# Block transposes on VectorE in the RWKV recurrence, and two gate projections moved into neighbouring jobs

## What is computed

```python
# first layer: 3592 columns of w_in; the last 8 are f_c, one per head
q_a, f_a, i_a, g_a, u_b, g_b, q_c, k_c, v_c, g_c, f_c = jnp.split(proj, IN_SPLIT_POINTS, axis=-1)
log_f_c = jax.nn.log_sigmoid((f_c + fox_f_bias[l]).astype(jnp.float32))
...
# second layer, RWKV: 16 heads of 64
def step(state, inp):
    r_t, w_t, k_t, v_t, a_t, b_t = inp
    sa = jnp.einsum('bhvk,bhk->bhv', state, a_t)
    state = (state * w_t[:, :, None, :] + sa[..., None] * b_t[:, :, None, :]
             + v_t[..., None] * k_t[:, :, None, :])
    return state, jnp.einsum('bhvk,bhk->bhv', state, r_t)
...
# second layer, NSA: the last 48 of its columns are gates (3 per head)
gates = jax.nn.sigmoid(gl.astype(f32)).reshape(B, S, G, HG, 3).transpose(0, 2, 3, 1, 4)
```

## Time and profile before

| | |
|---|---|
| time, median of 3 runs | 1584.03 us (1581.96 to 1585.93) |
| the profiled execution | 1581.26 us |
| its span | 1579.5 us |
| PE busy in the span | 1532.5 us (97%) |
| DVE / ACT / POOL busy | 894.6 / 695.7 / 120.6 us |
| mean granted TensorE clock | 0.992 |

### The profile page before, as it was taken

How to read it: one execution, slowest core, us unless ns; L and a number is a source line. 1 busy time by engine, 2 the same in 40 slices (tenths; PEclk the granted TensorE clock), 3 DMA queues, 4 the chain that set the end, 5 groups by cost and what they waited for, 6 DMA issues and landing times.

```text
span 1579.5 us, 33484 instructions
## 1 busy us (share of the span) xinstructions
PE 1532.5 (97%) x14426; PEld 1266.6 (80%) x14426; DVE 894.6 (57%) x1651; ACT 695.7 (44%) x1268; POOL 120.6 (8%) x86
## 2 busy tenths in 40 slices
PE   7999999899999999999999999999999999999998
PEld 6787867779789797897887677888887888888887
DVE  3658364656474574842245998433246677777323
ACT  5543264563352633524234998423235333333222
POOL 0004000002230322302000000000000000000000
PEclk9999989999999999999999999999999999999999
DMA  6322212431020110206312000223332323323231
GB/s 222 108 81 81 93 41 100 158 107 37 16 68 11 54 36 17 67 11 149 80 54 80 2 2 2 94 83 104 107 134 93 107 81 107 105 83 107 77 121 70
DMA packets 110978, 124.40 MB, mean 79 GB/s; under 512 B 21320, under 2 KB 94664, under 8 KB 110448
## 3 DMA queue, kind: packets, MB, share of 16 engines
q1 hardware_dynamic: 107904, 114.85, 23.1%
q10 hardware_dynamic: 2928, 7.41, 1.4%
HBM read 118.04 MB, written 4.21 MB: 77 GB/s over the span
## 4 chain that ended last, share of the span: by engine, by line
PE 84%; DVE 9%; ACT 5%; issue 2%; POOL 0%; DMA 0%; DVEq 0%; SPq 0%; ACTq 0%; POOLq 0%
PE bank L807 80%; PE bank L817 4%; ACT arena L1487 3%; DVE arena L2098 2%; DVE arena L2095 2%; DVE weights_lo L2095 1%; ACT L1487 1%; DVE arena L2102 1%; ACT weights_hi L1487 1%; DVE arena L2270 1%; DVE arena L2462 0%; DVE extra L2095 0%; DVE arena L2188 0%; DMA arena<-in_x 0%; ACT extra L1487 0%
## 5 line engine op out<-in xcount | busy, mean ns | idle before, releaser
L1487 ACT ACTIVATE arena<-bank 128x512 f32<-128x512 f32 (+3 forms) x415 | 225.3, 569 | 554.4 <-PE bank L807 528.0
L2095 DVE TENSOR_TENSOR weights_lo<-weights,weights_hi 128x1024 fp32r<-128x1024 f32 (+1 forms) x190 | 239.3, 1260 | 304.6 <-ACT weights_hi L1487 297.4
L807 PE MATMUL bank<-h_hi,weights_hi 128*128 128x512 f32 (+1 forms) x1008 | 400.8, 398 | 4.1 <-DVE h_lo L2098 1.9
L807 PE MATMUL bank<-h_lo,weights_hi 128*128 128x512 f32 (+1 forms) x1008 | 393.9, 391 | 0.0
L807 PE MATMUL bank<-h_hi,weights_lo 128*128 128x512 f32 (+1 forms) x1008 | 393.9, 391 | 0.0
L807 PE MATMUL bank<-arena 64*64 64x64 f32 (+6 forms) x7746 | 344.0, 247 | 14.7 <-DVE arena L2098 5.9
L807 PEld LDWEIGHTS bank<-arena 64*64 64x64 f32 (+3 forms) x7746 | 281.0, 140 | 68.2 <-issue 57.2
L1487 ACT ACTIVATE weights_hi<-weights 128x1024 fp32r<-128x1024 f32 (+1 forms) x190 | 200.1, 1053 | 172.3 <-PE bank L807 169.5
L807 PEld LDWEIGHTS bank<-h_hi,weights_hi 128*128 128x128 f32 (+1 forms) x1008 | 189.9, 188 | 50.8 <-issue 6.9
L807 PEld LDWEIGHTS bank<-h_hi,weights_lo 128*128 128x128 f32 (+1 forms) x1008 | 189.9, 188 | 40.6
L807 PEld LDWEIGHTS bank<-h_lo,weights_hi 128*128 128x128 f32 (+1 forms) x1008 | 190.0, 188 | 37.5
(11 more groups left out here) (172 smaller groups left out, 1628.2 us busy)
## 6 DMA issues: line engine op xcount, KB each, us to landing
weights<-in_w_in SPq DMA_DIRECT2D x39, 1024.0 KB, 5.3
weights<-in_ffn_up SPq DMA_DIRECT2D x22, 1024.0 KB, 5.1
weights<-in_ffn_down SPq DMA_DIRECT2D x10, 1024.0 KB, 5.0
weights<-in_w_out SPq DMA_DIRECT2D x8, 1024.0 KB, 5.0
weights<-in_w_in SPq DMA_DIRECT2D x16, 256.0 KB, 4.4
weights<-in_w_branch_rwkv SPq DMA_DIRECT2D x4, 1024.0 KB, 5.2
weights<-in_w_branch_nsa SPq DMA_DIRECT2D x4, 1024.0 KB, 5.2
weights<-in_w_in SPq DMA_DIRECT2D x5, 512.0 KB, 3.7
```

Of the source, the lines that this page charges most:

```text
L807: return pe.matmul(o, w, x, start=first, stop=last)
L1487: return act.activation(o, i, f, **kw)
L2095: return dve.tensor_tensor(o, a, b, op)
```

## The change

It has three parts.

1. In the RWKV solve the transposed powers are no longer made by matmuls. DVE transposes 32x32 blocks instead (`dve.transpose`, in the rows STREAM_TRANSPOSE, 128x512 each): `pw_even` into `ba` (twice per quarter), the results of `pa` 0 and `pa` 1 out of PSUM into `pwt` (four times), and `invt` into `inv` (four times). The jobs `pb`, `mx` and `mz` go, 8 groups of PE per quarter; `gram` loses the 64 columns from which `ba` was masked (384 instead of 512 per job). `bonus` moves behind `pa` 0. ACT's copy of `pa` 0 and 1 waits for DVE's transpose of the same bank.
2. The job `fc0` goes. Its 8 columns join the job `i` (264 columns); ACT copies them beside the values, and 4 small matmuls with the identity turn them (job `fc`, after `hk`). The gates' steps move from after `f0`, `q1` and `gb0` to after `i`, `gc0` and `gc1`, and SP's store and reload from ahead of `gc2`'s weights to ahead of `qc0`'s. The slots grow from 2048 to 2112 words, the pieces from 1024 to 1056.
3. The NSA gate job goes. Its 48 columns take 48 of the third lora job's 96 unused ones; ACT keeps them by one more copy (`keep`).

```diff
-        tokens(base["p1", "i"], w1, 512, 256)
+        tokens(base["p1", "i"], w1, None, 256 + FOX_HEADS, runs=((0, 512, 256), (256, 3584, FOX_HEADS)))
...
-        channels(base["lora"] + 2, (0, cols(w2, RWKV_COLS - P, RWKV_COLS)))
+        nb = RWKV_COLS
+        channels(base["lora"] + 2, (0, cols(w2, nb + 2560, nb + 2608)), (48, cols(w2, nb - 80, nb)))
...
-                if n == use_of[base["p1", "gc2"]]:
+                if n == use_of[base["p1", "qc0"]]:
...
-                    to_tokens(base["p1", name], h_both, 256)
+                    to_tokens(base["p1", name], h_both, 256 + FOX_HEADS)
                     pe.wait_ge(sem("hg_scaled"), 2)
                     for n in range(2):
                         transposes(base["hk"] + n, [hg_k[:, n, c * P:(c + 1) * P] for c in range(TT)])
+                    for i in range(TT):
+                        wait_read(pe, base["p1", "i"] + i)
+                    claim(pe, base["fc"])
+                    for i in range(TT):
+                        ins = mm(ps(base["fc"])[0:FOX_HEADS, i * P:(i + 1) * P], fc_tok[:, i, :], ident)
+                    fill(base["fc"], ins)
                 elif name == "v":
...
+                            at_ = 192 * n + DH * m
                             for x in range(2):
...
-                                    ins = mm(ps(j)[z, at_:at_ + P], src[both[x], n, tok], a_r[both[x], n, c, :, z])
+                                    if m:
+                                        ins = mm(ps(j)[z, at_:at_ + P], src[both[x], n, tok], a_r[both[x], n, c, :, z])
+                                    else:
+                                        ins = mm(ps(j)[z, at_:at_ + DH], src[both[x], n, tok], a_r[both[x], n, c, 1, z])
...
+
+                for g in range(2):
+                    pe.wait_ge(sem("powers_turned"), 6 * q + g + 1)
+                    pair_of_tiles(J[q, "pa", g, 0], g, ba, pw_even)
                 by_head(J[q, "bonus"], t1_q)
-
-
-                for g in range(2):
-                    pe.wait_ge(sem("powers_started"), 2 * q + g + 1)
-                    for c in (2 * g, 2 * g + 1):
-                        for x in range(2):
-                            wait_read(pe, J[q, "gram", c, x])
-                    pair_of_tiles(J[q, "pa", g, 0], g, ba, pw_even)
-                    pair_of_tiles(J[q, "pb", g, 0], g, pw_even, ba)
                 for g in range(2):
                     wait_read(pe, J[q, "pa", g, 0])
-                    wait_read(pe, J[q, "pb", g, 0])
+                    pe.wait_ge(sem("powers_turned"), 6 * q + g + 3)
                     pair_of_tiles(J[q, "pa", g, 1], g, pwt, pw_odd)
-                    pair_of_tiles(J[q, "pb", g, 1], g, pw_odd, pwt)
                     pe.wait_ge(sem("inv_started"), 2 * q + g + 1)
...
                 for g in range(2):
                     wait_read(pe, J[q, "pa", g, 1])
-                    wait_read(pe, J[q, "pb", g, 1])
+                    pe.wait_ge(sem("powers_turned"), 6 * q + g + 5)
                     pair_of_tiles(J[q, "pa", g, 2], g, pwt, pw_even)
...
                     pair_of_tiles(J[q, "pd", g, 3], g, pw_odd, invt)
+                    for c in (2 * g, 2 * g + 1):
+                        for x in range(2):
+                            wait_read(pe, J[q, "gram", c, x])
...
                     wait_read(pe, J[q, "pd", g, 3])
-                    turned(J[q, "mx", g], g, invt)
                     pe.wait_ge(sem("between_ready"), 4 * q + g + 1)
...
                 for g in range(2):
-                    wait_read(pe, J[q, "mx", g])
+                    pe.wait_ge(sem("inv_turned"), 4 * q + g + 1)
                     wait_read(pe, J[q, "mu", g, 0])
                     pair_of_tiles(J[q, "my", g, 0], g, inv, mid)
-                    pair_of_tiles(J[q, "mz", g], g, mid, inv)
                 for g in range(2):
                     wait_read(pe, J[q, "my", g, 0])
...
                 for g in range(2):
+                    pe.wait_ge(sem("inv_turned"), 4 * q + g + 3)
                     wait_read(pe, J[q, "mu", g, 1])
-                    wait_read(pe, J[q, "mz", g])
                     pair_of_tiles(J[q, "my", g, 1], g, inv, mid)
...
+            after_q = (nothing, lambda: hidden(0), lambda: hidden(1), block_keys, block_tokens, nothing, gate_tokens,
...
                     for i in range(TT):
-                        copy_out(j + i, hv_tok[:, i, :], width=256)
+                        wait_full(act, j + i)
+                        run(hv_tok[:, i, :], ps(j + i)[:, 0:256], ACT.Copy)
+                        read(j + i, run(fc_tok[:, i, :], ps(j + i)[:, 256:256 + FOX_HEADS], ACT.Copy))
...
+                    wait_full(act, base["fc"])
+                    read(base["fc"], run(fc_x[0:8, :], ps(base["fc"])[0:8, :], ACT.Identity, bias=params("fox_bias")[0:8]))
+                elif name == "gc0":
+                    act.wait_ge(sem("fox_abs"), 1)
+                    m = mark(run(fc_e[0:8, :], fc_abs[0:8, :], ACT.Exp, scale=-1.0))
+                    act.wait_ge(act_step, m)
+                    run(fc_e[0:8, :], fc_e[0:8, :], ACT.Ln, bias=1.0).then_inc(sem("fox_log"), 1)
...
+                if keep:
+                    run(gates_raw[0:48, :], ps(j)[0:48, :], ACT.Copy).then_inc(sem("gates_kept"), 1)
                 run(z_pad[:, m % 2, 1:513], ps(j), ACT.Copy)
                 read(j, run(z_c[:, m % 2, :], ps(j), ACT.Copy, scale=rest))
...
+                        if lev < 2:
+                            act.wait_ge(sem("powers_turned"), 6 * q + 2 * lev + g + 3)
...
+                    pool.wait_ge(sem("powers_turned"), 6 * q + g + 1)
+                    pool.tensor_tensor(part(invt, g), part(ba, g), over(m_one, 8), ALU.add).then_inc(sem("inv_started"), 1)
...
+                    if m:
+                        wait_full(pool, J[q, "bonus"])
...
                     tt(hg_q, hg_q, q_a, ALU.mult).then_inc(sem("hg_scaled"), 1)
                     tt(hg_k, hg_k, k_a, ALU.mult).then_inc(sem("hg_scaled"), 1)
+                    wait_read(dve, base["fc"])
+                    stt(a8, x8, -1.0, x8, ALU.mult, ALU.max).then_inc(sem("fox_abs"), 1)
...
+                    if name == "gc1":
+                        dve.wait_ge(sem("fox_log"), 1)
+                        then(stt(l8, x8, 0.0, e8, ALU.min, ALU.subtract))
+                        then(ts(a8, x8, 0.0, 1.0, ALU.mult, ALU.add))
+                        dve.tensor_tensor_scan(n8, a8, l8, 0.0, ALU.mult, ALU.add).then_inc(sem("fox_decay"), 1)
...
-                        read(j, tt(gram[:, c, x:4:2, :], ps(j).rearrange("p (n s) -> p n s", n=2), over(m_gram, 2),
+                        read(j, tt(gram[:, c, x:4:2, :], ps(j)[:, 0:384].rearrange("p (n s) -> p n s", n=2), over(m_gram, 2),
...
-                    j = J[q, "pb", g, lev]
+                    if c >= 2:
+                        g = c - 2
+                        dve.wait_ge(sem("powers_started"), 2 * q + g + 1)
+                        dve.transpose(flat(ba, g), flat(pw_even, g)).then_inc(sem("powers_turned"), 1)
...
+                def turn_power(g, lev):
+
+                    j = J[q, "pa", g, lev]
                     wait_full(dve, j)
-                    read(j, dve.tensor_copy(pwt[:, 2 * g:2 * g + 2].rearrange("p c h x -> p (c h x)"), ps(j)))
-
+                    dve.transpose(flat(pwt, g), ps(j)).then_inc(sem("powers_turned"), 1)
...
+                def turn_inverse(j, g):
+
+                    wait_read(dve, j)
+                    dve.transpose(flat(inv, g), flat(invt, g)).then_inc(sem("inv_turned"), 1)
+
+                for g in range(2):
+                    turn_power(g, 0)
                 j = J[q, "bonus"]
                 wait_full(dve, j)
                 read(j, dve.tensor_copy(bonus, ps(j)[:, 0:16]))
-                for g in range(2):
...
                     sum_into(J[q, "pd", g, 3], g, invt)
+                    turn_inverse(J[q, "pd", g, 3], g)
                 for g in range(2):
                     wait_read(dve, J[q, "pd", g, 3])
                     sum_into(J[q, "my", g, 0], g, invt)
...
                 for g in range(2):
-                    wait_read(dve, J[q, "my", g, 0])
+                    turn_inverse(J[q, "my", g, 0], g)
+                for g in range(2):
+                    wait_full(dve, J[q, "mu", g, 1])
                     sum_into(J[q, "my", g, 1], g, invt)
```

More of the change, by code:

```diff
@@ L92 @@
 LN_TINY = -69.07755278982137
-P1 = ("fc0", "f0", "f1", "q0", "q1", "ga0", "ga1", "gb0", "gb1", "i", "gc0", "gc1", "gc2", "gc3",
+P1 = ("f0", "f1", "q0", "q1", "ga0", "ga1", "gb0", "gb1", "i", "gc0", "gc1", "gc2", "gc3",
       "u0", "u1", "qc0", "qc1", "qc2", "qc3", "kc0", "kc1", "kc2", "kc3", "v")
@@ L239, in build_program @@
         at += 48
-        gram = view(at, TT, 4, 256)
-        pw_even, invt, inv, mid = (view(at + 4096 + 1024 * n, TT, 4, DH) for n in range(4))
+        gram, ba = view(at, TT, 4, 192), view(at + 3072, TT, 4, DH)
+        pw_even, invt, e_late, inv = (view(at + 4096 + 1024 * n, TT, 4, DH) for n in range(4))
```

(22 more changed lines are left out.)

87 lines of the change are left out of this document (22 added, 65 removed).

## The result

The changed kernel takes 1563.94 us in the median (1556.63 to 1573.99, 4 runs) where the kernel before takes 1582.99 (1580.28 to 1585.93, 4 runs). The ratio is 0.989, with an interval of [0.9867, 0.9914]: 17.4 us faster (14 to 21), where 28 were forecast. The time lies in the range of 1547 to 1565, at its upper end; the ratio applied to 1584.03 is 1566.6, just beyond it. The direction was right, over a third of the gain was missing.

The account below looks back on a forecast made before the run. PE was taken as the bound, busy 1532.5 of 1579.5 us. The terms -3.8 - 2.7 + 1.25 + 1.05 - 5.5 + 0.5 - 23.8 + 5 = -28.0 took 1584.03 to 1556.0 us, range 1547 to 1565.

Parts of the forecast that it names:

- `fc0`, `i` and the gates: First layer: earlier `f0` -3.8 us, wait before `i` gone -2.7, added matmul work +1.25, waits at the gates' new place +1.05.
- The start of `f0`: First layer: with `fc0` out, `f0` starts at about 18.2 instead of 23.14, held by its loads; net -3.8 us.
- the wait at `i`: First layer: PE's wait of 2.73 us before `i`, for DVE's low part, goes: -2.7 us.
- the wait at `gc2`: First layer: the gates' moved steps on ACT and DVE make PE wait about 0.55 us before `gc2`.
- `gc3`: First layer: the gates' 8x512 steps on DVE make PE wait some 0.5 us before this job.
- The NSA job and the copy: NSA gate job's 24 matmuls gone, -5.5 us; one extra ACT copy on the chain to `decay`, +0.5.
- The solve: RWKV solve: eight groups fewer per quarter, less waits at the first powers; savings 6.3, 6.7, 5.4 and 5.4, together -23.8 us.
- The transpose: RWKV solve: one DVE transpose of 128x512 taken to cost 0.61 us, like a copy; the skill's figures gave 0.7.
- (a): Rival, RWKV solve: transposes cost 1.22 us, adding 1.85 per quarter, +7.4 in all, giving 1563.4; chance 0.10.
- (c): Rival, RWKV solve: the transpose takes four passes, 2.3 us, adding 10.9 per quarter, +43.6, giving 1599.6; chance 0.05.
- (b): Rival, first layer: dropping `fc0` gives nothing, so 3.8 + 2.7 us are not had, giving 1562.5; chance 0.08.
- The clock: RWKV quarters: new waits lower TensorE's clock twice in four quarters, +5 us; bounds 0 and +13.6.

Follow-up runs that it names:

- e1: The kernel before with only slots widened to 2112 words and pieces to 1056: 1590.6 us against 1581.8, ratio 1.0056.
- e5: The kernel before with only the second high part moved, to 1056 words behind the first instead of 1024: 1591.94 us against 1582.96, ratio 1.0061.
- e6: The changed kernel with the second high part 1088 words behind the first instead of 1056: 1551.61 us, ratio 0.9806 to the kernel before.
- e4: The kernel before with only the NSA gates' part of the change: 1577.89 us, ratio 0.9972.
- e12: e6 with each of the 40 block transposes made twice, one behind the other: 1568.94 us against 1580.7 for the kernel before, ratio 0.9922.
- e7: e6 with `bonus` put back ahead of the first powers: 1547.05 us, ratio 0.9772 to the kernel before.
- e10: The kernel before with slots and high parts together 32 words further on, activations left in place: 1598.92 us in one execution.

## Why the prediction missed, point by point

- **The step that failed** is the widening of slots and pieces from 2048 and 1024 words to 2112 and 1056. It stands in the change and has no term in the sum: matmuls that stay were taken to cost what they cost before. What costs is the second high part, 1056 words behind the first, 32 off a multiple of 64. It costs 9 us in the kernel before (e1, e5) and 13 in the changed one, clock included (e6). Without it the forecast of -28.0 meets -30.7.
- **A sign that was there.** The sum takes 0.2317 as the distance of two matmuls at full clock, from the 24 of the gate job. The ordinary jobs beside it have 0.2267 (5.44 / 24). In the gate job the weights lie 48 columns, so 48 words, apart from one contraction step to the next, and in `fc0` 104, so that most do not start at a multiple of 64. That fits the effect; no run separates it from the smaller number of columns. Asking why this row was 2% slower might have led to the missing term.
- **`fc0`, `i` and the gates.** Forecast -3.8 - 2.7 + 1.25 + 1.05 = -4.2. The attention's first matmul of 2 columns starts at 201.79 before and at 196.72 in e6: -5.1. The start of `f0`, the wait at `i` and the wait at `gc2` came as worked out; `gc3` had 0.3 instead of 0.5. The job `i` takes 11.62 before, 11.66 after and 11.62 in e6, where +0.35 was forecast, and `fc` took 0.97 (forecast 0.9).
- **The NSA job and the copy.** Forecast -5.0, measured -4.4. The idle time ahead of `decay` grew from 0.27 to 0.56, and to 0.73 in e4.
- **The solve.** Forecast -5.4 for quarter 2 at full clock. From `ta` of quarter 1 to `ta` of quarter 2 are 587.96 - 489.98 = 97.98 before and 567.10 - 474.21 = 92.89 in e6: -5.1. From `ta` of 0 to `ta` of 1: 100.19 and 94.18, -6.0 (forecast 5.4 to 6.7). Part 1 alone gives -20.4, where -23.8 + 5 = -18.8 was forecast.
- **The transpose.** I took 0.61 from the copy; it is 0.62 in a queue. The estimate of 0.7 worked out from the Trainium skill ("VectorE: DVE Perf Modes", the three transpose paths, and "Vector Engine (DVE) Microarchitecture Reference", section 3.8) meets the single instruction, 0.70. Rivals (a) and (c) fall by that, and (b) by the row at 18.19. The price that (a) puts on a transpose of twice the length, 1.85 per quarter, was too high for the transposes themselves and left out the clock (e12).
- **The clock.** +5 is about right on the mean, in part by luck, and wrong in its spread. Over the four runs of the changed kernel the mean clock is 0.977, 0.983, 0.991 and 0.993, and the times are 1573.99, 1568.31, 1559.57 and 1556.63: 17.4 us for 0.016. Their mean of 0.986 against 0.991 of before makes 0.005 x 17.4 / 0.016 = 5.4 us. The working had one fall of 3.4 and one of 6.8 in the quarters; the profiled execution has 17.0 us of low clock there. The bounds of 0 and +13.6 were those of the quarters alone, but the falls come elsewhere too (298 to 306, 786 to 792, where before has none behind the same waits), and the profiled execution has 47 us more of low clock than that of before (71 against 24).
- **The reading of the waits.** Behind equal waits quarter 2 keeps its clock and quarter 3 loses it for 10.2 us; the Trainium skill ("TensorE: Matmul & The Clock Gate", on oscillation), by whose rule on idle gaps all quarters would fall, is borne out for some of these gaps of 1.1 to 1.4 us and not for others. What decides was not found. Run e12 shows more low clock with longer waits, and e7 shows that taking these waits away does not raise the mean clock.

## What to carry to other kernels

When an edit moves or widens a buffer from which TensorE reads, compare the spacing of matmuls that were not changed, in a stretch without waits, before anything else is explained: 1.2% there was 12 us, where the whole change was to bring 28. Try the distance between weights and activations as a number of its own; here 0 and 64 words are free and 32 costs 3% of a job. And where work of PE with no successor near (here `bonus`) stands behind a new wait, put it in the wait. When two kernels are compared stretch by stretch, look at the granted clock of both stretches before the difference is given a cause.

## What the runs showed of the hardware

- Matmuls of 512 columns with 128x128 weights slow down from 0.2267 to up to 0.234 us each with the place of the weights in SBUF. With the high part moved against the rest, 24 of them take 5.44 us at 0, 4 and 64 words, 5.56 at 8, 5.59 at 16, 5.61 at 32 and 96, 5.49 at 48. With weights and activations moved together by 32 words they take 5.44. The clock was granted in full, PE waited for nothing, and it is the same while no other engine and no DMA is at work (0.2325 in e10, 0.2267 before).
- A VectorE transpose of 32x32 blocks takes 0.68 to 0.72 us for 128x512 fp32, out of SBUF or PSUM, and 0.62 from start to start in a queue.
- TensorE's clock can fall behind waits of 0.4 to 1.4 us that stand close together, and then stay at its low level for about 3.4, 6.8 or 10.2 us; equal waits in the same execution leave it up (quarters 2 and 3 of the changed kernel). Between executions of one kernel this made 17 us.
